# VectorE instead of GpSimd computes the low parts of the output projection's weights in an attention stage

## The chip, the cores and the metric

The kernel runs on one core of a Trainium2 chip. The metric is device time in microseconds of one execution. One profiled execution of the kernel before gives the trace that is read here. In the trace and below, PE is TensorE (PEld its weight loads), DVE is VectorE, ACT is ScalarE and POOL is GpSimd.

## The reference

One layer of a hybrid decoder is computed for 1024 prompt tokens and 64 sample tokens (8 sequences of 8), all in float32, model width 1024:

```python
def _decoder_layer(x, ...):
    x = _layer_norm(DN_ALPHA * x + 0.5 * _swiglu(x, f1g, f1u, f1d), ...)
    m, s_new, new_k, new_v = _mixer(x, w_in, w_out, gn_w, sinks, ...)
    x = _layer_norm(DN_ALPHA * x + m, ...)
    x = _layer_norm(DN_ALPHA * x + 0.5 * _swiglu(x, f2g, f2u, f2d), ...)

def _mixer(h, w_in, w_out, gn_w, sinks, ...):
    rq, rk, rv, rg, sq, sk, sv = _project_in(h, w_in)
    o_ret, s_new = _retention(rq, rk, rv, s0, RET_CHUNK)
    o_swa = _swa_prompt(sq, sk, sv, sinks)          # window 128, ALiBi, sinks
    y_ret = silu(rg) * _head_group_norm(o_ret, gn_w)
    merged = concatenate([y_ret, o_swa], axis=-1)
    return merged @ w_out, s_new, new_k, new_v
```

The sliding-window attention has 8 query heads on 2 key/value heads. Each block of 128 queries sees its own 128 keys and the 128 before; a learned sink per head joins maximum and denominator of the softmax.

## The kernel before

The layer is a row of stages. Large products are made from float32 numbers that are split in two: a high part, rounded by ACT, and a low part, the raw number minus the high part. A product is high x high + low x high + high x low, so each weight tile needs one rounding and one subtraction before use.

`attention_stage` has a block of its own, and ahead of it and behind it all engines meet. The next block begins with `output_projection_stage`, whose products use `out_weights`. These are eight raw tiles of 128x1024 (`ow_raw`), rounded by `OutWeights.round` on ACT (L1490, to `ow_hi`) and split by `OutWeights.split` (L1494, to `ow_low`). Both run inside the attention stage; the projection's TensorE program waits for all eight low parts before its first product.

The stage works on 18 items: 8 prompt blocks and the sample tokens, each for 2 key/value heads. Items 0 and 1 have no block before theirs and are half as wide; 2 to 15 are whole; 16 and 17 are the samples. An item passes the engines so:

- PE `score` (L1599): scores of 4 heads into PSUM
- DVE `add_bias` (L1670), then `top` (the maximum L1678, and three small operations on 128x4 statistics, L1680, L1682, L1683)
- ACT `exponentials` (L1724)
- DVE `denominator` (L1687, L1689)
- POOL (L1785): the scores times the inverse denominator, in place. It is called norm here
- PE `transposes` (L1619), ACT `read_turned` (L1745), PE `output` (L1640)
- ACT `high_part` (L1760), DVE `low_part` (L1704): the result in two parts

Each engine runs an order written out by hand:

- PE: scores of items 0 to 3; then for each i: transposes(i), score(i+4), output(i-1)
- DVE: for each i from -4: add_bias(i+4), top(i+4), denominator(i+3), low_part(i-2)
- ACT: exponentials 0 to 3; then for each i: read_turned(i), exponentials(i+4), high_part(i-1), and for i below 8 round of weight tile i
- POOL: for each i: norm(i), and for i from 1 to 8 split of weight tile i-1, which waits for that tile's rounding

There are four score buffers (`SLOTS = 4`), two sets of score banks, and two of turned tiles. SP (the DMA queue) loads bias tables, caches and the eight raw tiles at the stage's start and stores the new caches.

Of the kernel before, what the change touches and what calls it, by code (L numbers as in the profile page):

```python
# [22 lines left out]
F32 = mybir.dt.float32  # L23
F32R = mybir.dt.float32r
ACT = mybir.ActivationFunctionType
ALU = mybir.AluOpType
# [5 lines left out]
KT = D_MODEL // P  # L32
# [168 lines left out]
def ffn_stage(core, tag, buffers, w_in, fold, acc, xh, xl, wait_x, acc_ready, norm, room=None, banks_free=None,  # L201
# [161 lines left out]
    def gpsimd_early(pool):  # L363
        split(pool, 0, 0, GATE)
        split(pool, 0, 0, UP)

    def gpsimd(pool):
        def step(f, s):
            split(pool, f + 1, 1 - s, GATE)
            split(pool, f + 1, 1 - s, UP)  # L370
            split(pool, f, s, DOWN)

        step(0, 0)
        if prefetch:
            prefetch.gpsimd_early(pool)
        tiles(pool, step)
        split(pool, B, 1, GATE)
        split(pool, B, 1, UP)
        split(pool, A, 0, DOWN)
        split(pool, B, 1, DOWN)  # L380
        for t in range(7):
            norm.gain(pool, t)
# [1090 lines left out]
class OutWeights:  # L1473
# [15 lines left out]
        act.wait_ge(self.staged[k // 2], 32)  # L1489
        act.activation(self.hi[k][:, :], self.raw[k][:, :], ACT.Copy).then_inc(self.hi_done, 1)  # L1490

    def split(self, pool, k):
        pool.wait_ge(self.hi_done, k + 1)
        pool.tensor_tensor(self.low[k][:, :], self.raw[k][:, :], self.hi[k][:, :].bitcast(F32),  # L1494
                           ALU.subtract).then_inc(self.lo_done, 1)


def attention_stage(core, at, at_caches, tables, sinks, sinks_dec, caches, q_t, k_t, v_tok, ident,
# [36 lines left out]
    def shape(i):  # L1535

        n, h = ITEMS[i]
        if n == BLOCKS:
            return 2, 0, KEYS
        return GROUP, (P if n == 0 else 0), 2 * P  # L1540

    def scores_of(i):
        n, h = ITEMS[i]
        groups, k0, k1 = shape(i)
        width = KEYS if n == BLOCKS else 2 * P
        return scores[i % SLOTS][:, 0:groups * width].rearrange("p (g k) -> p g k", g=groups)[:, :, k0:k1]

    def per_group(i, what):
        return stats[i % SLOTS][:, what, 0:shape(i)[0]]

    def sinks_of(i):
        n, h = ITEMS[i]
        if n == BLOCKS:
            return sinks_dec[:, h:h + 1].to_broadcast([P, 2])
        return sinks[:, GROUP * h:GROUP * h + GROUP]
# [98 lines left out]
    def vector(dve):  # L1654
        def add_bias(i):
            n, h = ITEMS[i]
            groups, k0, k1 = shape(i)
            dve.wait_ge(tables_in if n == BLOCKS else bias_in[h], 16)
            dve.wait_ge(scored, i + 1)
            if i >= SLOTS:  # L1660
                dve.wait_ge(turn_done, i - SLOTS + 1)
            out = scores_of(i)
            if n == BLOCKS:
                ps = score_ps[i % 2][0][:, 0:2 * KEYS].rearrange("p (g k) -> p g k", g=2)
                dve.scalar_tensor_tensor(out, ps, QSCALE, bias_dec[:, h, :, :], ALU.mult, ALU.add)\
                   .then_inc(biased, 1)
            else:
                for j in range(2):
                    ps = score_ps[i % 2][j][:, :].rearrange("p (g k) -> p g k", g=2)[:, :, k0:k1]
                    x = dve.scalar_tensor_tensor(out[:, 2 * j:2 * j + 2, :], ps, QSCALE,  # L1670
                                                 bias[:, h, 2 * j:2 * j + 2, k0:k1], ALU.mult, ALU.add)
                x.then_inc(biased, 1)

        def top(i):
            dve.wait_ge(biased, i + 1)
            if i >= SLOTS:
                dve.wait_ge(normed, i - SLOTS + 1)
            dve.tensor_reduce(per_group(i, TOP), scores_of(i), AX.X, ALU.max).then_inc(maxed, 1)  # L1678
            dve.wait_ge(maxed, i + 1)
            dve.tensor_tensor(per_group(i, TOP), per_group(i, TOP), sinks_of(i), ALU.max).then_inc(topped, 1)  # L1680
            dve.wait_ge(topped, i + 1)
            dve.tensor_tensor(per_group(i, SINK), sinks_of(i), per_group(i, TOP), ALU.subtract)  # L1682
            dve.tensor_scalar(per_group(i, NEG), per_group(i, TOP), -1.0, None, ALU.mult).then_inc(negated, 1)  # L1683

        def denominator(i):
            dve.wait_ge(sink_exped, i + 1)
            dve.tensor_tensor(per_group(i, DEN), per_group(i, SUM), per_group(i, SINK), ALU.add).then_inc(summed, 1)  # L1687
            dve.wait_ge(summed, i + 1)
            dve.reciprocal(per_group(i, INV), per_group(i, DEN)).then_inc(inverted, 1)  # L1689

        def low_part(i):
            n, h = ITEMS[i]
            d = slice(HD * h, HD * h + HD)
            dve.wait_ge(hi_done, i + 1)
            if n == BLOCKS:
                for t in range(GROUP):
                    x = dve.tensor_tensor(
                        mix_lo[d, PAIRS + t, SEQ:TOK].rearrange("p (b i) -> p b i", i=DEC_SEQ),
                        out_ps[h][d, 0:2 * P].rearrange("p (b t i) -> p b t i", t=GROUP, i=DEC_SEQ)[:, :, t, :],
                        mix_hi[d, PAIRS + t, SEQ:TOK].rearrange("p (b i) -> p b i", i=DEC_SEQ).bitcast(F32),  # L1700
                        ALU.subtract)
                x.then_inc(lo_done, 1)
            else:
                dve.tensor_tensor(mix_lo[d, PAIRS:2 * PAIRS, P * n:P * n + P],  # L1704
                                  out_ps[h][d, :].rearrange("p (t q) -> p t q", t=GROUP),
                                  mix_hi[d, PAIRS:2 * PAIRS, P * n:P * n + P].bitcast(F32),
                                  ALU.subtract).then_inc(lo_done, 1)

        for i in range(-SLOTS, LAST + 2):
            if i + SLOTS < LAST:  # L1710
                add_bias(i + SLOTS)
                top(i + SLOTS)
            if 0 <= i + SLOTS - 1 < LAST:
                denominator(i + SLOTS - 1)
            if i >= 2:
                low_part(i - 2)

    def scalar(act):
        def exponentials(i):
# [55 lines left out]
    def gpsimd(pool):  # L1775
        for t in range(GROUP):
            pool.tensor_copy(q_rows[:, :, t, :], q_t[:, t, SEQ:TOK].rearrange("p (b i) -> p b i", i=DEC_SEQ))\
                .then_inc(q_ordered, 1)
        pool.memset(turned_new[:, :], 0.0).then_inc(q_ordered, 1)
        for i in range(LAST):  # L1780
            n, h = ITEMS[i]
            groups, k0, k1 = shape(i)
            pool.wait_ge(inverted, i + 1)
            s = scores_of(i)
            pool.tensor_tensor(s, s, per_group(i, INV).unsqueeze(2).to_broadcast([P, groups, k1 - k0]),  # L1785
                               ALU.mult).then_inc(normed, 1)
            if 1 <= i <= KT:
                out_weights.split(pool, i - 1)

    return Stage(sync=sync, tensor=tensor, vector=vector, scalar=scalar, gpsimd=gpsimd)  # L1790


# [109 lines left out]
def decoder_layer(core, i, o):  # L1902
# [84 lines left out]
    with nc.Block() as block:  # L1987
# [48 lines left out]
        def _(pe):  # L2036
# [5 lines left out]
        core, att_end, mix_lo_att_at, gates_end, i["gn_sum"], i["gn_spread"], ones_head, eps, part("gn_w"), ret_q, ret_gate,  # L2042
        mix_hi, mix_lo, i["w_att"], xh, xl, ident, att_q, att_k, att_v_tok, retention.outputs_stored))
    one_stage_block(nc, attention_stage(core, att_end, mixer_at, i, part("sinks"), part("sinks_dec"),
                                        {"k": i["k_cache"], "v": i["v_cache"]}, att_q, att_k, att_v_tok, ident,
                                        mix_hi, mix_lo, o, out_weights))
# [202 lines left out]
```

## Time and profile before

| what | value |
|---|---|
| time, median of 3 runs | 2267.71 us (2265.05 to 2269.71) |
| the profiled execution's own time | 2266.3 us |
| its span, first to last instruction | 2264.4 us |
| PE busy | 2197.3 us (97% of the span) |
| PEld busy | 1978.2 us (87%) |
| DVE busy | 892.3 us (39%) |
| ACT busy | 510.6 us (23%) |
| POOL busy | 520.2 us (23%) |
| attention stage | from about 1217 to 1340 us of the span |

The span is 1.9 us shorter than the execution's time; that is what lies around it. Busy shares are means over all stages. The attention stage lies in slices 22 to 24 of the 40 that the profile's page draws (each 56.6 us), and in those PE is below nine tenths and its granted clock is below full speed.

### The profile page before, as it was taken

The numbers are of one execution on the slowest core, as the hardware profiler recorded it, in microseconds if no ns is written. First come the engines' busy times: TensorE is split into PE (matmuls) and PEld (weight loads), VectorE is DVE, ScalarE is ACT, GpSimd is POOL, SyncE is SP. The second block draws the span as 40 slices with busy tenths as digits, with TensorE's granted clock in tenths as the row PEclk, the third lists the DMA queues.
The fourth block names the chain that finished last, engine by engine and source line by source line (L and its number), as shares of the span: only waits on it lengthen the run. The fifth ranks groups of instructions, "written<-read, shape, count | busy, mean of one in ns | idle before, by whom it ended". The sixth has DMA issues, their size and how long they took to land. (4 is left out here: it accounts for less than half of the span.)

```text
span 2264.4 us, 31134 instructions
## 1 busy us (share of the span) xinstructions
PE 2197.3 (97%) x12045; PEld 1978.2 (87%) x12045; DVE 892.3 (39%) x1606; ACT 510.6 (23%) x877; POOL 520.2 (23%) x253
## 2 busy tenths in 40 slices
PE   8999999999999999999898889999999999999997
PEld 8999999999999889996676458799999999999996
DVE  5534434344344430012133543433443434435246
ACT  4111111111111431111123542311111111111115
POOL 4121221212212222213122522222112121221213
PEclk9999999999999999999697699999999999999999
DMA  7101011010111011110103030010101101010112
GB/s 271 56 28 56 28 56 49 34 56 28 56 42 52 29 70 66 37 32 21 65 10 140 0 114 3 29 56 28 56 28 56 46 37 56 28 56 28 56 57 79
DMA packets 37817, 118.42 MB, mean 52 GB/s; under 512 B 5879, under 2 KB 10615, under 8 KB 37503
## 3 DMA queue, kind: packets, MB, share of 16 engines
q1 hardware_dynamic: 37759, 117.61, 14.6%
q8 instruction: 41, 0.67, 0.1%
q14 instruction: 17, 0.14, 0.0%
HBM read 106.32 MB, written 11.27 MB: 52 GB/s over the span
## 5 line engine op out<-in xcount | busy, mean ns | idle before, releaser
L111 PE MATMUL bank<-x_hi,f_w_hi 128*128 128x362 f32 (+1 forms) x2104 | 688.3, 327 | 7.0 <-issue 5.6
L113 PE MATMUL bank<-x_hi,f_w_low 128*128 128x362 f32 (+1 forms) x2104 | 689.9, 328 | 0.0
L360 POOL TENSOR_TENSOR f_w_low<-f_w_raw,f_w_hi 128x1024 fp32r<-128x1024 f32 x132 | 317.3, 2418 | 1177.5 <-ACT f_w_hi L290 1177.5
L548 DVE TENSOR_TENSOR acc<-bank,acc 128x512 f32<-128x512 f32 x720 | 468.0, 687 | 7.0 <-PE bank L446 5.8
L111 PEld LDWEIGHTS bank<-x_hi,f_w_hi 128*128 128x128 f32 x2104 | 396.4, 188 | 9.1 <-issue 7.4
L113 PEld LDWEIGHTS bank<-x_hi,f_w_low 128*128 128x128 f32 x2104 | 395.9, 188 | 0.0
L526 DVE TENSOR_TENSOR f_h_full<-bank,f_silu 128x362 f32<-128x362 f32 (+1 forms) x132 | 70.7, 535 | 816.9 <-PE bank L113 814.6
L112 PE MATMUL bank<-x_lo,f_w_hi 128*128 128x362 f32 (+1 forms) x1056 | 345.3, 327 | 0.0
L112 PE MATMUL bank<-x_low,f_w_hi 128*128 128x362 f32 (+1 forms) x1048 | 342.9, 327 | 0.0
L444 PE MATMUL bank<-f_w_hi,f_h_hi 128*128 128x512 f32 x640 | 250.8, 392 | 0.1
L446 PE MATMUL bank<-f_w_low,f_h_hi 128*128 128x512 f32 x640 | 250.1, 391 | 0.0
L445 PE MATMUL bank<-f_w_hi,f_h_lo 128*128 128x512 f32 x640 | 249.9, 390 | 0.0
L299 ACT ACTIVATE f_silu<-bank 128x362 f32<-128x362 f32 (+1 forms) x132 | 62.5, 474 | 682.4 <-PE bank L113 682.4
L112 PEld LDWEIGHTS bank<-x_lo,f_w_hi 128*128 128x128 f32 x1056 | 198.9, 188 | 0.9
L112 PEld LDWEIGHTS bank<-x_low,f_w_hi 128*128 128x128 f32 x1048 | 197.2, 188 | 0.8
L305 ACT ACTIVATE f_h_hi<-f_h_full 128x362 fp32r<-128x362 f32 (+1 forms) x132 | 67.0, 508 | 528.8 <-DVE f_h_full L526 528.8
L446 PEld LDWEIGHTS bank<-f_w_low,f_h_hi 128*128 128x128 f32 x640 | 120.1, 188 | 26.7
L444 PEld LDWEIGHTS bank<-f_w_hi,f_h_hi 128*128 128x128 f32 x640 | 120.1, 188 | 25.1 <-issue 0.8
L445 PEld LDWEIGHTS bank<-f_w_hi,f_h_lo 128*128 128x128 f32 x640 | 120.1, 188 | 24.6
L290 ACT ACTIVATE f_w_hi<-f_w_raw 128x1024 fp32r<-128x1024 f32 x132 | 134.0, 1044 | 32.3 <-DMA f_w_raw<-ffn_in 32.3
L111 PE MATMUL bank<-x_hi,rp_w_hi 128*128 128x362 f32 (+1 forms) x384 | 127.0, 331 | 3.9 <-ACTq L908 3.9
L113 PE MATMUL bank<-x_hi,rp_w_low 128*128 128x362 f32 (+1 forms) x384 | 126.3, 329 | 0.0
(192 smaller groups left out, 2347.7 us busy)
## 6 DMA issues: line engine op xcount, KB each, us to landing
f_w_raw<-ffn_in SPq DMA_DIRECT2D x132, 512.0 KB, 4.4
rp_w_raw<-w_ret_in SPq DMA_DIRECT2D x16, 512.0 KB, 3.5
acc<-x_rows_in SPq DMA_DIRECT2D x2, 2048.0 KB, 11.1
kept_rows<-acc SPq DMA_DIRECT2D x8, 512.0 KB, 3.0
ow_raw<-w_out_in SPq DMA_DIRECT2D x8, 512.0 KB, 11.3
y_out<-acc SPq DMA_DIRECT2D x8, 512.0 KB, 2.6
n_rows<-ln_rows_in SPq DMA_DIRECT2D x6, 512.0 KB, 7.8
gp_stage<-w_att_in SPq DMA_DIRECT2D x6, 512.0 KB, 3.4
```

Of the source, the lines that this page charges most:

```text
L111: pe.matmul(out, wh, xh, start=first, stop=False)
L112: pe.matmul(out, wh, xl, start=False, stop=False)
L113: return pe.matmul(out, wl, xh, start=False, stop=last)
L290: act.activation(flat(w_hi[s][j]), flat(w_raw[s][j]), ACT.Copy).then_inc(down_hi if j == DOWN else gu_hi, 1)
L299: act.activation(silu[:, buffer_of(f, s, c), 0:b - a], gate_ps[pair_of(f, s, c)][:, 0:b - a], ACT.Silu).then_inc(silu_done, 1)
L305: act.activation(h_hi[s][:, a:b], h_full[:, buffer_of(f, s, c), 0:b - a], ACT.Copy).then_inc(h_hi_done, 1)
L360: pool.tensor_tensor(flat(w_lo[s][j]), flat(w_raw[s][j]), flat(w_hi[s][j]).bitcast(F32), ALU.subtract).then_inc(done, 1)
L444: pe.matmul(out, h_hi[s][:, u], hi, start=True, stop=False)
L445: pe.matmul(out, h_lo[s][:, u], hi, start=False, stop=False)
L446: pe.matmul(out, h_hi[s][:, u], lo, start=False, stop=True).then_inc(down_done, 1)
L526: dve.tensor_tensor(h_full[:, at, 0:b - a], up_ps[pair_of(f, s, c)][:, 0:b - a], silu[:, at, 0:b - a], ALU.mult).then_inc(pair_free, 1)
L548: dve.tensor_tensor(acc[:, t, d], down_ps[(n + 2 * s) % 4][:, :], acc[:, t, d], ALU.add).then_inc(down_free, 1)
```

## The change

`split` is called on DVE instead of POOL. On POOL the call behind norm(i), for i from 1 to 8, is gone. On DVE it stands at the end of the loop's round i, behind low_part(i-2), and still waits for the rounding of weight tile i-1. Operands, their shapes, the semaphores and their counts are the same.

```diff
-    def split(self, pool, k):
-        pool.wait_ge(self.hi_done, k + 1)
-        pool.tensor_tensor(self.low[k][:, :], self.raw[k][:, :], self.hi[k][:, :].bitcast(F32),
-                           ALU.subtract).then_inc(self.lo_done, 1)
+    def split(self, dve, k):
+        dve.wait_ge(self.hi_done, k + 1)
+        dve.tensor_tensor(self.low[k][:, :], self.raw[k][:, :], self.hi[k][:, :].bitcast(F32),
+                          ALU.subtract).then_inc(self.lo_done, 1)
...
             if i >= 2:
                 low_part(i - 2)
+            if 1 <= i <= KT:
+                out_weights.split(dve, i - 1)
...
                                ALU.mult).then_inc(normed, 1)
-            if 1 <= i <= KT:
-                out_weights.split(pool, i - 1)
-
```

## Rows read from the trace of the kernel before

**Rows 1.** The page's head.
```profile
span 2264.4 us, 31134 instructions
```

**Rows 2.** Windows: stretch and length; each engine's busy us (instructions); PEclk; DMA share; GB/s.
```profile
1242.85:1307.58 64.73, 56.45 (x158) 30.18 (x158) 37.05 (x70) 36.78 (x103) 33.13 (x16) 0.69 0.00 1
1307.58:1322.56 14.98, 13.53 (x85) 7.55 (x84) 12.10 (x33) 11.18 (x37) 6.43 (x4) 1.00 0.01 1
```

**Rows 3.** Timeline: start, duration (us), engine, line, operation, shapes, count, idle before and releaser.
```profile
1251.74 0.18 DVE L1689 RECIPROCAL at_stats<-at_stats 128x4 f32<-128x4 f32 x1
...
1263.82 2.34 POOL L1494 TENSOR_TENSOR ow_low<-ow_raw,ow_hi 128x1024 fp32r<-128x1024 f32 x1 [4.00 <-ACT ow_hi L1490]
1266.13 1.89 POOL L1785 TENSOR_TENSOR at_scores<-at_scores,at_stats 128x1024 f32<-128x1024 f32 x1
1268.07 1.09 PE L1619 MATMUL bank<-small,at_scores 128*128 128x128 f32 x8 [3.32 <-POOL at_scores L1785]
...
1279.18 1.04 ACT L1490 ACTIVATE ow_hi<-ow_raw 128x1024 fp32r<-128x1024 f32 x1
1280.30 2.35 POOL L1494 TENSOR_TENSOR ow_low<-ow_raw,ow_hi 128x1024 fp32r<-128x1024 f32 x1 [4.00 <-ACT ow_hi L1490]
```

**Rows 4.** Waits: who waited for whom, us in total, times, longest.
```profile
PEld bank L1619 <- POOL at_scores L1785: 20.1, 8, 4.2
```

**Rows 5.** Two lines of DVE subtractions: ns least/median/most, first and last start, forms.
```profile
L159 DVE TENSOR_TENSOR x_low<-x_raw,x_hi x6: 902/1694/3194, 6.4 to 21.0; 128x724 fp32r<-128x724 f32 x4, 128x2912 fp32r<-128x2912 f32 x1, 128x2896 fp32r<-128x2896 f32 x1
L534 DVE TENSOR_TENSOR f_h_lo<-f_h_full,f_h_hi x132: 457/537/2795, 25.2 to 2237.3; 128x362 fp32r<-128x362 f32 x44, 128x364 fp32r<-128x364 f32 x44, 128x298 fp32r<-128x298 f32 x44
```

**Rows 6.** A line's least/median/most ns, then timeline of DVE and POOL operations that overlap.
```profile
L1682 DVE TENSOR_TENSOR at_stats<-small,at_stats x18: 160/162/1817, 1222.7 to 1326.0; 128x4 f32<-128x4 f32 x16, 128x2 f32<-128x2 f32 x2
...
1266.22 1.82 DVE L1682 TENSOR_TENSOR at_stats<-small,at_stats 128x4 f32<-128x4 f32 x1
1418.99 1.28 DVE L711 SCALAR_TENSOR_TENSOR acc<-acc,n_stats,n_rows 128x1024 f32<-128x1024 f32 x1
1419.47 3.06 POOL L689 TENSOR_TENSOR acc<-acc,n_rows 128x1024 f32<-128x1024 f32 x1 [9.04 <-ACT acc L682]
```

**Rows 7.** Timeline of DVE's loop round i = 9, and the norm it releases.
```profile
1305.89 1.29 DVE L1670 SCALAR_TENSOR_TENSOR at_scores<-bank,at_bias 128x512 f32<-128x512 f32 x2 [1.92 <-PE bank L1599]
1309.01 0.18 DVE L1689 RECIPROCAL at_stats<-at_stats 128x4 f32<-128x4 f32 x1
1309.22 0.69 DVE L1704 TENSOR_TENSOR mix_lo<-bank,mix_hi 64x512 fp32r<-64x512 f32 x1
1309.26 1.89 POOL L1785 TENSOR_TENSOR at_scores<-at_scores,at_stats 128x1024 f32<-128x1024 f32 x1 [3.89 <-DVE at_stats L1689]
```

**Rows 8.** Timeline of PE, two items: later one first, at the lower clock.
```profile
1292.83 1.97 PE L1619 MATMUL bank<-small,at_scores 128*128 128x128 f32 x8 [0.78 <-POOL at_scores L1785]
1294.73 3.78 PE L1599 MATMUL bank<-att_k,att_q 64*128 64x256 f32 x8
1298.44 3.67 PE L1640 MATMUL bank<-at_turned,att_v_tok 128*64 128x512 f32 x4
...
1277.37 1.99 PE L1599 MATMUL bank<-att_k,att_q 64*128 64x256 f32 x8
1279.29 1.93 PE L1640 MATMUL bank<-at_turned,att_v_tok 128*64 128x512 f32 x4
```

**Rows 9.** Windows, columns as in group 2: where the granted clock moves, and later.
```profile
1258.00:1260.00 2.00, 1.96 (x4) 0.36 (x3) 1.90 (x5) 0.00 (x0) 1.82 (x1) 0.70 0.00 0
1268.00:1270.00 2.00, 1.93 (x11) 1.65 (x12) 0.93 (x5) 1.85 (x7) 0.02 (x1) 0.86 0.00 0
1303.60:1338.00 34.40, 32.45 (x210) 17.69 (x210) 20.07 (x54) 24.34 (x77) 11.00 (x7) 1.00 0.01 1
```

**Rows 10.** Timeline around the first split: output(0) on PE, add_bias(5) on DVE.
```profile
1239.50 1.97 PE L1640 MATMUL bank<-at_turned,att_v_tok 128*64 128x512 f32 x2
1239.67 1.29 DVE L1670 SCALAR_TENSOR_TENSOR at_scores<-bank,at_bias 128x512 f32<-128x512 f32 x2 [4.03 <-PE bank L1599]
```

## The prediction

> **What bounds the kernel now.** I read the page's head first: the span is 2264.4 us [rows 1], 1.9 us under the execution's own 2266.3 us. PE is busy for 97% of it, so anything worth having in this change lies in the one stage that the diff touches, where PE is not full. The windows show that stage in two halves [rows 2]. From 1242.85 us (the transposes of item 2) to 1307.58 (those of item 10) eight items take 64.73 us, 8.1 us each, at a mean granted clock of 0.69. Behind them, from 1307.58 to 1322.56, three items take 14.98 us, 5.0 us each, at the full clock. The first half is the one in which weight tiles are rounded and split.
>
> Then the timeline of that half, to see what turns it [rows 3]. One ring closes over two items: the split of tile 3 starts at 1263.82 on POOL; behind it norm(5) runs from 1266.13; PE, idle for 3.32 us, starts transposes(5) at 1268.07, when norm(5) ends; then come score(9), add_bias(9), its maximum and exponentials, high_part(4), ACT's rounding of tile 5 at 1279.18, and the split of tile 5 at 1280.30. That is 16.48 us for two items. norm(5) needed nothing from this ring: item 5 had its inverse denominator at 1251.9. It stood in POOL's queue behind a split that waits for a rounding, which stands in ACT's queue behind the exponentials of an item four further on. The list of waits shows the price: PE's weight loads for the transposes waited for norm 8 times, 20.1 us together [rows 4], and these gaps also cost clock (below). The split's 2.35 us is the smaller half of its harm; its wait is the larger.
>
> **What goes.** POOL loses 8 x 2.35 us and 8 waits. Norm(i) then starts as soon as its denominator is there, two to three items ahead of its transposes, and is no longer late for PE. In these eight items POOL keeps 1.89 us an item.
>
> **What comes, on DVE.** Eight subtractions of 128x1024 with both inputs in SBUF. The trace before has no such shape on DVE. The nearest rows are 0.902 us for 724 columns and 0.537 for 362 [rows 5], 1.01 ns a column, which gives 1.20 us for 1024; the step from 298 to 362 columns (0.457 to 0.537, 1.25 ns a column) would give 1.37. I take 1.22, nearer to the wider row. The new wait for the rounding is free: ACT rounds tile i-1 straight behind high_part(i-2), and DVE stands behind low_part(i-2), 0.69 us of work, and (next step) behind a norm as well. Were it not, add_bias and top of the next item would be queued behind it, and with them ACT's exponentials.
>
> The costly part is when the subtraction may run. DVE's small two-input operation at 1266.22 took 1.82 us where the median of its line is 0.162, and ended with the norm of 1266.13; the other way round, POOL's addition that came up at 1419.47, while a DVE operation of 1.28 us had been running since 1418.99, took 3.06 us: 0.80 us of waiting and 2.26 of its own [rows 6]. So such operations take turns. Where would the split fall? DVE's round i = 9 shows it [rows 7]: add_bias starts at 1305.89, the reciprocal ends at 1309.19, which releases a norm at 1309.26 to 1311.15, and low_part ends at 1309.91. A split there would find the norm running, start at about 1311.2 and end at 1312.4. The round would take 1312.4 - 1305.9 = 6.5 us, against 4.0 without the split (1309.9 - 1305.9) and 5.2 with a split that met nobody.
>
> The Trainium skill's page "SBUF — State Buffer", section "Who interferes with whom", says the same: a VectorE instruction with two SBUF inputs contends with a GpSimd instruction that reads SBUF, and who is first keeps the port for the whole instruction. It speaks against moving this operation to VectorE; by it the split costs VectorE 2.5 us an item, and by instruction length alone 1.2.
>
> **PE and ACT beside it.** Gapless, an item costs PE at the lower clock 1.97 for transposes, 3.78 for the score and 3.67 for the output, less an overlap of 0.07 at each of the three seams (1292.83 + 1.97 is 0.07 beyond 1294.73): 9.2 us [rows 8]. At the full clock it is 1.09 + 1.99 + 1.93 less the same, 4.8 us [rows 3, 8]. ACT was busy for 36.78 us in eight items, 4.6 us each [rows 2], the rounding included. So at the full clock DVE's 6.5 us sets the pace, at the lower one PE's 9.2.
>
> The clock rose from 1.2 to 2.4 GHz in the window 1258 to 1260, in which PE was busy for 1.96 of 2 us; it fell in the window 1268 to 1270, behind the gap of 3.32 us; from 1303.6 to 1338 PE was busy for 32.45 of 34.40 us and it stayed at full [rows 9]. In the new kernel PE works without a gap as long as it is the slower one, so the clock should rise in item 2, 3 or 4; afterwards PE idles 6.5 - 4.8 = 1.7 us an item, in a gap half as long as the one behind which it fell. I take it that it stays up.
>
> **The sum.** Nothing changes up to output(0) at 1239.50 and add_bias(5) at 1239.67 [rows 10]. Transposes(2) then follow output(0) at 1241.5 instead of 1242.85. With score(6) still at the lower clock (1.90 + 3.70), add_bias(6) starts at 1247.2 From there seven rounds of 6.5 us lead to add_bias(13) at 1247.2 + 45.5 = 1292.7. Before, that was 1305.89 [rows 7]: 13.2 us earlier. Behind it both kernels run the same rounds at about 5 us, and the stage's end and the whole projection follow as much earlier. 2266.3 - 13.2 = 2253.1 us. The median of the runs shown is 1.4 us above this execution (2254.5 by it); I forecast 2254.0.
>
> Bounds of this sum: clock up within item 2, as early as transposes(2): 2.5 us more gain; clock up one or two items later: 9.2 - 6.5 = 2.7 us less gain each; the subtraction at 1.37 us: 7 x 0.15 = 1 us less. The next block starts with its own clock step, which can fall otherwise by 1 or 2 us. So 2249 to 2260.
>
> **Rivals.**
> A. The subtraction does not meet the norm (it goes first, or they don't exclude each other at this shape). A round is 5.2 us: 7 x 1.3 = 9 us more, 2244 us. Against it: [rows 6, 7]. 6%.
> B. The clock keeps swinging as before, because of the 1.7 us gaps, or rises three to six items late: half of the seven rounds at 9.2 us cost 9.5 us, gain 4 us, 2262 to 2267. For it: before, the clock rose and fell within these items and its mean was 0.69 [rows 2, 9]. Against it: the gaps are half as long. 9%.
> C. The clock stays at 1.2 GHz through all seven rounds. PE is then the bound: add_bias(13) at 1247.2 + 7 x 9.2 = 1311.6, 5.7 us later than before, 2272 us, slower. It decides from the fifth slow round on (13.2 / 2.7 = 4.9). For it: at the item of 1292.83 to 1302 the clock was still low, although PE had been busy for most of the stretch before [rows 2, 8]. Against it: PE is without a gap there, and before, it rose in such a stretch [rows 9]. 6%.
>
> **Chances.** Forecast 79%, A 6%, B 9%, C 6%. The median before tells 0.2% (4.5 us), about what a measurement of this kernel can tell from no change. Faster by more than that, under 2263.2: forecast, A and little of B, 85%; the same: most of B, 9%; slower: C, 6%. The range for 8 in 10 is 2248 to 2261: the forecast's own bounds, and a bit of either side.
>
> **What the profile after would show.** Norm with no wait for a split, PE's waits for norm gone; ow_low on DVE x8 at about 2.4 us each (1.2 of it standing behind a norm); add_bias starts 6.5 us apart for items 6 to 13; clock at 1.00 from about 1250 on; DVE's small operations on statistics back at 0.16 us. Starts about 5.2 us apart would speak for A, a clock under 0.9 between 1250 and 1290 for B or C. The forecast is wrong if the stage's end moves by under 8 us or over 18.

## The result, and the profile after

The changed kernel takes 2247.60 us (median of 4 runs, 2243.67 to 2249.86); the kernel before took 2268.11 us beside it (4 runs, 2265.05 to 2269.71). The ratio is 0.9909, with an interval of 0.9896 to 0.9922. The profiled execution took 2248.2 us, against 2266.3. So the gain is 18 us in the profiled pair and 20.5 in the medians, where 13.2 was forecast. The time lies 0.4 us under the lower end of the range. That is less than the kernel's own spread: its repetition a1, below, has 2250.01 us, which lies inside.

The page's head, and its lines of busy time and granted clock (tenths in 40 slices) after the change:

```profile
span 2246.4 us, 31134 instructions
...
PE 2182.5 (97%) x12045; PEld 1973.3 (88%) x12045; DVE 895.3 (40%) x1614; ACT 510.4 (23%) x877; POOL 508.5 (23%) x245
...
PEclk9999999999999999999698899999999999999999
```

VectorE has only 3 us more to do than before, although it took over eight whole tiles, 12.9 us of splits: it got most of that back from two small operations, L1680 and L1682, which had stood waiting for 8.9 us in all. The window from transposes(2) to transposes(10), columns as in [rows 2], is 47.80 us long where it was 64.73, and its clock rose from 0.69 to 0.91:

```profile
1240.66:1288.46 47.80, 42.03 (x160) 23.66 (x159) 41.91 (x80) 36.65 (x103) 21.97 (x8) 0.91 0.00 1
```

The waits that answer to [rows 4], with the total in us, the number and the longest. Two of the waits for norm are left, ahead of items 1 and 15. In items 2 to 9, which had seven of the eight waits before (19.3 of the 20.1 us), there is none. There PE now waits for ACT's reading of the turned tile.

```profile
PEld bank L1619 <- POOL at_scores L1787: 4.0, 2, 3.2
PE bank L1619 <- ACT at_turned L1747: 9.5, 8, 2.5
```

Two rounds of the changed kernel, from the timeline of VectorE and GpSimd (they answer to [rows 3, 7]; norm is now L1787):

```profile
1257.46 1.22 DVE L1678 TENSOR_REDUCE at_stats<-at_scores 128x4 f32<-128x1024 f32 x1
1258.91 0.16 DVE L1682 TENSOR_TENSOR at_stats<-small,at_stats 128x4 f32<-128x4 f32 x1
1259.34 0.65 DVE L1704 TENSOR_TENSOR mix_lo<-bank,mix_hi 64x512 fp32r<-64x512 f32 x1
1259.51 3.38 POOL L1787 TENSOR_TENSOR at_scores<-at_scores,at_stats 128x1024 f32<-128x1024 f32 x1 [4.49 <-DVE at_stats L1689]
1259.92 1.21 DVE L1494 TENSOR_TENSOR ow_low<-ow_raw,ow_hi 128x1024 fp32r<-128x1024 f32 x1
1261.05 1.27 DVE L1670 SCALAR_TENSOR_TENSOR at_scores<-bank,at_bias 128x512 f32<-128x512 f32 x2
...
1264.36 0.69 DVE L1704 TENSOR_TENSOR mix_lo<-bank,mix_hi 64x512 fp32r<-64x512 f32 x1
1264.41 1.89 POOL L1787 TENSOR_TENSOR at_scores<-at_scores,at_stats 128x1024 f32<-128x1024 f32 x1 [1.53 <-DVE at_stats L1689]
1265.09 2.30 DVE L1494 TENSOR_TENSOR ow_low<-ow_raw,ow_hi 128x1024 fp32r<-128x1024 f32 x1
1267.42 1.29 DVE L1670 SCALAR_TENSOR_TENSOR at_scores<-bank,at_bias 128x512 f32<-128x512 f32 x2
```

Norm and split meet in every round, as forecast, and take turns. But in one round the split goes through in 1.21 us and norm is stretched to 3.38, and in the next norm takes its 1.89 and the split 2.30. The rounds last 6.37 and 4.92 us in turn: 11.29 us for two, not 13.0.

A yardstick for all that follows is the stretch from add_bias(5) to add_bias(13), eight rounds. Before: 1239.67 to 1305.89, 66.2 us [rows 7, 10]. After: 1238.92 to 1286.76, 47.8 us. That is 18.4 us less, about the whole gain of the profiled pair: the changed kernel came to this stretch 0.7 us earlier, and lost 1.1 us again behind the stage. The forecast had 53.0 (1292.7 - 1239.67).

### The profile page after: what moved, and what is told of

Same layout as the page of the kernel before. It is cut to its first block and busy times, and to the rows that moved or that the text cites. A ratio compares the mean times of both kernels' runs of the same rounds, so it can differ in the third digit from the quotient of the medians.

```text
span 2246.4 us, 31134 instructions
## 1 busy us (share of the span) xinstructions
PE 2182.5 (97%) x12045; PEld 1973.3 (88%) x12045; DVE 895.3 (40%) x1614; ACT 510.4 (23%) x877; POOL 508.5 (23%) x245
## 5 line engine op out<-in xcount | busy, mean ns | idle before, releaser
L112 PE MATMUL bank<-x_low,rp_w_hi 128*128 128x362 f32 (+1 forms) x384 | 126.5, 330 | 0.0
## 6 DMA issues: line engine op xcount, KB each, us to landing
ow_raw<-w_out_in SPq DMA_DIRECT2D x8, 512.0 KB, 11.3
```

The costliest lines, as they stand in the source:

```text
L112: pe.matmul(out, wh, xl, start=False, stop=False)
```

## Experiments

Each kernel is the changed one or the one before with a single edit, unless said otherwise. The table gathers them: "eight rounds" is the yardstick read from each timeline, "clock falls" those inside it. The kernel before had, beside a1, e1, e2 and e4, a median of 2267.93 us (9 runs), beside e7 to e10 2268.52 (13 runs), beside e5 and e6 a single 2272.85, beside t2 to t4 a single 2267.99.

| kernel | time, us | ratio to before [interval] | eight rounds, us | clock falls |
|---|---|---|---|---|
| before | 2268.11 | | 66.2 | swings throughout |
| changed | 2247.60 | 0.9909 [0.9896, 0.9922] | 47.8 | 1 |
| a1, changed again | 2250.01 | 0.9912 [0.9895, 0.9929] | 49.5 | 2 |
| e1 | 2245.26 | 0.9900 [0.9881, 0.9920] | 44.5 | 0 |
| e2 | 2248.41 | 0.9915 [0.9899, 0.9932] | 46.2 | 1 |
| e4 | 2250.05 | 0.9921 [0.9902, 0.9939] | 49.5 | 2 |
| e5 / e6 | 2259.92 / 2262.00 (one execution each) | | 60.5 / 60.5 | 2 / 1 |
| e7 | 2267.36 | 0.9994 [0.9984, 1.0004] | 64.3 | 0 from 1260 us on |
| e8 | 2242.28 | 0.9883 [0.9866, 0.9899] | 43.0 | 1, short |
| e9 | 2254.73 | 0.9942 [0.9926, 0.9959] | 53.6 | 3 |
| e10 | 2241.68 | 0.9881 [0.9864, 0.9897] | 40.6 | 0 |
| t2 / t3 / t4 | 2249.53 / 2248.34 / 2248.15 (one execution each) | | 50.5 / 47.9 / 49.7 | 1 / 1 / 2 |

**a1, the changed kernel once more.** It gives the spread of the changed kernel itself.

> The changed kernel once more, as a yardstick beside the variants. Expected: 18 to 22 us below the kernel before (2246 to 2250 us), ow_low alternately about 1.2 and 2.3 us long on DVE, longest pauses of PE about 1.4 to 1.8 us. If the gain of 20 us were chance of one chip, it would come out at 13.

The ratio repeats. The same kernel had two clock falls instead of one, and 1.7 us more in the eight rounds.

**e2, was it the place in the queue or the engine?** The kernel before, GpSimd keeps all splits, but each stands behind a later norm, when its rounding is long done:

```diff
-            if 1 <= i <= KT:
-                out_weights.split(pool, i - 1)
+            if 4 <= i < KT + 4:
+                out_weights.split(pool, i - 4)
```

> The kernel before, with all splits on GpSimd, but that of tile i-4 behind norm(i), for i from 4 to 11, in place of tile i-1 for i from 1 to 8. The rounding is then done long before. Theory W (the wait and where it stands is what costs): norm is never late, DVE's statistics are never held for long, and the kernel is as fast as the changed one or up to 3 us faster, 2244 to 2249 us, although GpSimd does just as much. Theory L (GpSimd's length costs: 2.35 + 1.89 us an item, during which DVE's two-input operations stand): DVE's statistics are held by 1 to 2 us an item, and it stays above 2255 us.

```profile
1261.31 0.16 DVE L1682 TENSOR_TENSOR at_stats<-small,at_stats 128x4 f32<-128x4 f32 x1
1261.91 1.89 POOL L1785 TENSOR_TENSOR at_scores<-at_scores,at_stats 128x1024 f32<-128x1024 f32 x1 [2.99 <-DVE at_stats L1689]
1263.76 2.37 POOL L1494 TENSOR_TENSOR ow_low<-ow_raw,ow_hi 128x1024 fp32r<-128x1024 f32 x1
1266.18 0.16 DVE L1682 TENSOR_TENSOR at_stats<-small,at_stats 128x4 f32<-128x4 f32 x1
```

GpSimd's splits cost 2.35 to 2.37 us as before, and yet the time is that of the changed kernel. Norm follows its denominator, the split has no wait, and no small operation of VectorE is held (L1682 takes 0.16 us throughout). What the change brings, it brings by moving the wait out from ahead of norm, not by using a faster engine.

**e4, what do the splits cost VectorE?** The changed kernel without any split. The projection waits for the high parts alone and uses them in place of the low parts too, so its output is another one.

> The splits are left out and the projection's third product takes the high part of the weights a second time (same count of products, other numbers). What the splits still cost in the changed kernel. If only the port and DVE's time bind there, a round falls to the 5.0 to 5.4 us that PE and ACT need, 3 to 4 us less in all: 2244 to 2246 us, equal to the two variants. If DVE were the sole bound, DVE rounds of 4.0 us: over 8 us less, under 2240 us.

The time is that of the changed kernel, where 3 to 4 us less was expected. Without a single split VectorE's round is as short as it can be, and still the rounds are 4.81 and 6.44 us (add_bias at 1257.88, 1262.69, 1269.13, 1273.94): 11.25 us for two. So the changed kernel is not bound by VectorE's 6.5 us a round, which was my step. A ring over two items binds it.

**e1, what if the split never loses the port?** The split goes ahead of `low_part` in VectorE's round, where it starts before norm:

```diff
-            if i >= 2:
-                low_part(i - 2)
             if 1 <= i <= KT:
                 out_weights.split(dve, i - 1)
+            if i >= 2:
+                low_part(i - 2)
```

> DVE does the split ahead of low_part instead of behind it. Theory H (hold): behind a low_part of partitions 64 to 127 the split, which starts at partition 0, is held until low_part has ended, and the norm, released by the reciprocal, gets the port first; behind a low_part of partitions 0 to 63 it isn't held and gets the port first. With nothing between reciprocal and split, all eight splits then take about 1.2 us and all eight norms beside them 2.8 to 3.4 us; add_bias starts 5.0 to 5.7 us apart, the stage ends 3 us earlier than in the changed kernel, 2244 to 2246 us. Theory C (a cycle of two rounds in the timing, whatever lies between): splits stay alternately at 1.2 and 2.3 us, and the time is that of the changed kernel.

```profile
1258.12 1.19 DVE L1494 TENSOR_TENSOR ow_low<-ow_raw,ow_hi 128x1024 fp32r<-128x1024 f32 x1
1258.28 2.78 POOL L1787 TENSOR_TENSOR at_scores<-at_scores,at_stats 128x1024 f32<-128x1024 f32 x1 [3.48 <-DVE at_stats L1689]
...
1263.02 1.20 DVE L1494 TENSOR_TENSOR ow_low<-ow_raw,ow_hi 128x1024 fp32r<-128x1024 f32 x1
1263.08 1.06 PE L1619 MATMUL bank<-small,at_scores 128*128 128x128 f32 x8 [1.13 <-ACT at_turned L1747]
1263.19 2.78 POOL L1787 TENSOR_TENSOR at_scores<-at_scores,at_stats 128x1024 f32<-128x1024 f32 x1 [2.12 <-DVE at_stats L1689]
```

A window of e1, columns as in [rows 2]:

```profile
1242.00:1316.00 74.00, 65.60 (x354) 36.74 (x352) 54.19 (x125) 57.06 (x168) 30.68 (x14) 1.00 0.00 1
```

All splits take 1.2 us, and the pace stays (add_bias at 1248.66, 1254.90, 1259.83, 1266.16: 11.2 us for two). PE's pause ahead of the transposes of items 3 to 9 is 1.13 us at most where the changed kernel shows up to 1.73, and in this window the clock never falls. Both halves of the expectation for H came out, the short splits and the time; theory C did not. The 3.3 us less in the eight rounds are about the price of the changed kernel's one fall (3.1, below). In the medians e1 is 2.3 us under the changed kernel; their intervals overlap.

**The ring of the changed kernel.** From its timeline, over two items: transposes at 1264.31, score 1265.30, add_bias 1267.42, maximum 1268.74, exponentials 1270.47, high_part 1272.66, rounding 1273.28, read_turned 1274.36, transposes 1275.59. That is 11.28 us, through PE, DVE and ACT.

```profile
1264.31 1.06 PE L1619 MATMUL bank<-small,at_scores 128*128 128x128 f32 x8 [1.73 <-ACT at_turned L1747]
...
1273.28 1.06 ACT L1490 ACTIVATE ow_hi<-ow_raw 128x1024 fp32r<-128x1024 f32 x1
1274.36 1.08 ACT L1747 ACTIVATE at_turned<-bank 128x512 f32<-128x512 f32 x2
1275.59 1.06 PE L1619 MATMUL bank<-small,at_scores 128*128 128x128 f32 x8 [1.63 <-ACT at_turned L1747]
```

The rounding of a weight tile stands in ACT's queue between two of its links. If this ring binds, rounding elsewhere must shorten two rounds by about 1.0 us, to 10.3.

**e8 and e10, the rounding out of the ring.** e8 is e1, e10 is e2, each with this edit in ACT's loop:

```diff
             if i < LAST:
                 read_turned(i)
+            if i < KT:
+                out_weights.round(act, i)
             if i + SLOTS < LAST:
                 exponentials(i + SLOTS)
             if i:
                 high_part(i - 1)
-            if i < KT:
-                out_weights.round(act, i)
```

> The variant with the split ahead of low_part, and on ACT the rounding of tile i directly behind read_turned(i), ahead of exponentials(i+4), where ACT waits for DVE's statistics anyway. Theory R (the changed kernel is bound by a ring over two items through all engines: transposes, score, add_bias, maximum, exponentials, high_part, rounding, read_turned, transposes, 11.3 us): 1.04 us of rounding leaves the ring, rounds fall from 5.6 to about 5.2 us, which is then DVE with its split; 3 us less than the variant before it, 2242 to 2245 us. Theory D (DVE's rounds are the bound already): no change against it, 2245 to 2248 us.

> Splits on GpSimd, late (tile i-4 behind norm(i), for i from 4 to 11), and the rounding ahead of exponentials(i+4). No step of the weights is left in any ring; rounds of 5.0 us set by PE, ACT and the statistics. The fastest of all: 2241 to 2244 us. If GpSimd's 4.24 us an item hold DVE's statistics at the port, 2246 us or more.

e8: rounds of 5.25 and 4.95 us, 10.2 for two. e10: 5.36 and 4.81 (add_bias at 1255.90, 1260.71, 1266.07), 10.17 for two, with the splits on GpSimd. Both agree with the ring. e10, at 2241.68 us, has the lowest median of the study, not told apart from e8's; all its executions are below all of the changed kernel's, and it doesn't contain the change.

**What bound the kernel before?** The forecast named a ring over two items through PE, 16.48 us. Read again, the same stretch of the trace before has a shorter one, over one item and without PE: split at 1263.82; norm 1266.13 to 1268.02; VectorE's small operation L1682, held from 1266.22 to 1268.04 [rows 6]; and then, from the timeline of the kernel before (its last line, of the next item, is explained below):

```profile
1268.15 0.51 ACT L1724 ACTIVATE at_scores<-at_scores,at_stats 128x256 f32<-128x256 f32 x1 [3.45 <-DVE at_stats L1683]
1270.35 0.59 ACT L1760 ACTIVATE mix_hi<-bank 64x512 fp32r<-64x512 f32 x1
1270.96 1.06 ACT L1490 ACTIVATE ow_hi<-ow_raw 128x1024 fp32r<-128x1024 f32 x1
...
1272.10 2.35 POOL L1494 TENSOR_TENSOR ow_low<-ow_raw,ow_hi 128x1024 fp32r<-128x1024 f32 x1 [4.08 <-ACT ow_hi L1490]
...
1275.22 1.09 DVE L1680 TENSOR_TENSOR at_stats<-at_stats,small 128x4 f32<-128x4 f32 x1
```

Exponentials, high_part, rounding, next split: 1272.10 - 1263.82 = 8.28 us an item. The link that I had missed is a 128x4 operation that waits for norm at the port. In the next item it is L1680 that is held: it comes up at 1275.22 and ends at 1276.31, with the norm of 1274.40 to 1276.29. Twice 8.28 is 16.56, so my ring had nearly the same length. But it reaches the statistics through add_bias(9) at 1272.65, and L1680 of that item could have been done 0.9 us sooner than the norm let it: my ring had slack there. Both rings contain exponentials, high_part and rounding. e7 tells them apart, and with them the clock; e9 takes the link out that they share.

**e7, more work and a full clock.** The kernel before with the output products of items 2 to 8 computed twice into the same bank:

```diff
-                for kb in range(first, 2):
-                    mm = pe.matmul(out_ps[h][d, :], ...)
+                for turn in range(2 if 2 <= i <= 8 else 1):
+                    for kb in range(first, 2):
+                        mm = pe.matmul(out_ps[h][d, :], ...)
```

> The kernel before, in which PE issues the products of output(i) twice for items 2 to 8 (the second pass starts anew and gives the same numbers), into its idle stretches: 7 x 1.9 us more PE work at the full clock. It asks what the low clock cost. The granted clock should stay near 1.0 from item 3 on. Theory S (PE's steps lie in the ring of the kernel before, as the prediction had it): transposes of 1.09 us in place of 1.97 and scores of 1.99 in place of 3.5 shorten every ring of two items by 1.5 us or more, 4 to 6 us less in all. Theory P (the ring runs GpSimd's split, norm, DVE's held statistics, ACT's exponentials, high_part, rounding, 8.2 us an item, with no PE step in it): rounds stay at 8.2 us, time the same within 3 us, or a little longer.

A window, and three lines of the timeline:

```profile
1260.00:1308.00 48.00, 41.65 (x156) 20.97 (x155) 33.77 (x55) 28.45 (x83) 26.15 (x13) 1.00 0.00 1
```

```profile
1271.58 2.36 POOL L1494 TENSOR_TENSOR ow_low<-ow_raw,ow_hi 128x1024 fp32r<-128x1024 f32 x1 [4.28 <-ACT ow_hi L1490]
1273.89 1.89 POOL L1786 TENSOR_TENSOR at_scores<-at_scores,at_stats 128x1024 f32<-128x1024 f32 x1
1273.99 1.82 DVE L1683 TENSOR_TENSOR at_stats<-small,at_stats 128x4 f32<-128x4 f32 x1
```

The clock is 1.00 for 48 us, the transposes take 1.09 us each, and the splits still start at 1263.10, 1271.58, 1279.60, 1287.88 and 1295.89, 8.0 to 8.5 us apart. The time doesn't change (0.9994, within 0.16% either way). PE's own part of my ring, from transposes(5) to add_bias(9), shrank from 4.58 us (1268.07 to 1272.65) to 3.11 (1267.45 to 1270.56), and the pace of the splits stayed at 8.3 us. So neither PE's work nor its low clock set the pace before: the ring through the port did. Only behind the last split did the full clock count: the eight rounds are 1.9 us shorter than before, 1.7 of them between that split and add_bias(13).

**e9, the kernel before with the rounding early.** Only e8's edit of ACT, splits as before.

> The kernel before, splits on GpSimd as they were, with only ACT's rounding moved ahead of exponentials(i+4). If the wait for the rounding is what closes the ring of the kernel before (split waits for rounding, rounding for exponentials, these for statistics that stand behind GpSimd's norm at the port, norm behind the split), the ring opens: about 10 us less, 2255 to 2260 us. If GpSimd's length is what costs (2.35 + 1.89 us an item), nothing changes: 2266 to 2270 us.

13.8 us less than before, a little more than was expected, without touching any split or GpSimd. Small operations are still held (L1682: 1.82 us at 1256.12) and GpSimd still waits for roundings (4.97, 0.53, 4.77, 0.53 us in turn), but the rounding no longer stands behind exponentials and high_part, and the ring opens: 6.7 us a round. That is still longer than the changed kernel's 5.6 in undisturbed rounds; norm still stands behind a split here, and I take that for the reason, without a run that shows it.

**Who gets the port?** In the changed kernel the split wins in every second round. `low_part` writes partitions 0 to 63 for one key/value head and 64 to 127 for the other; the split, on all 128, starts at partition 0. Hypothesis (H in the expectations): an operation that starts at other partitions than the one ahead is held until that one has ended, and the held split loses the port to norm. The start times fit: behind `low_part` on 0 to 63 the split starts 0.07 us before its end (1259.92 against 1259.99), behind 64 to 127 0.04 after (1265.09 against 1265.05). e5 and e6 cut every split in two halves of 64 partitions. For tiles 2, 4 and 6, whose `low_part` ahead lies on partitions 64 to 127, e5 puts the upper half first and e6 the lower one; the other tiles have the lower half first in both:

```diff
-        dve.tensor_tensor(self.low[k][:, :], ...)
+        for h in (1, 0) if k in (2, 4, 6) else (0, 1):     # e6: (0, 1) for all
+            p = slice(HD * h, HD * h + HD)
+            x = dve.tensor_tensor(self.low[k][p, :], ...)
```

> The changed kernel with each split done in two operations of 64 partitions, 1.2 us each; for tiles 2, 4 and 6, whose low_part in front of them lies on partitions 64 to 127, the upper half goes first. Theory H (an operation that starts at another partition than the one before it is held until that one has ended): the upper half isn't held behind low_part, DVE gets the port first in all eight rounds, the norms of all eight rounds wait for it (2.8 us or more), and no half of a split is longer than about 1.3 us. Theory C (the order at the port alternates by timing alone): norms of 1.89 us appear in some of the rounds of tiles 2, 4 and 6 with a first half of about 2.3 us.

> The same with the lower half first for every tile: the same two operations and the same time on DVE, only the order of the halves differs for tiles 2, 4 and 6. Theory H: behind the low_parts of partitions 64 to 127 the lower half is held, the norm goes first (1.89 us) and the first half of tiles 2, 4 and 6 takes about 2.3 us. Theory C: as in the variant with the upper half first.

H's expectation for e5 failed. For e6 it came out in tiles 2, 4 and 6 (norm 1.89 us, first half 2.29), but the other tiles lose there too. Norm keeps its 1.89 us from the second round on in both kernels, also where the first half is not held (in e5 at 1257.06, 0.07 us before `low_part`'s end): a pair of halves then takes 3.52 to 3.79 us, which is two operations at the whole one's 1.2 us and a wait for norm. All rounds from add_bias(6) on are 7.6 us. Two things could spoil this test: two operations in place of one, or 64 partitions. t4 cuts by columns instead, two operations of 128x512:

```diff
-        dve.tensor_tensor(self.low[k][:, :], ...)
+        for c in (slice(0, 512), slice(512, 1024)):
+            x = dve.tensor_tensor(self.low[k][:, c], ...)
```

> The changed kernel with each split in two operations of 128 partitions and 512 columns, about 0.65 us each. In the two variants that split by partitions the norm went first in every round from the second on. If the partitions (64 in place of 128) were the reason, DVE gets the port first here in every second round, as in the changed kernel (norms of 2.5 us or more there). If the reason is that the operation that waits for the rounding is no longer the one that signals the end, or that there are two, the norm goes first here too, 1.89 us in all these rounds.

From the second on the pairs take 1.27 us with norm at 3.45, and 2.36 with norm at 1.90, in turn, as in the changed kernel. So it is not the count of operations; a form with 64 partitions loses. Why it does stays open. t2 and t3 leave the split whole and put a 64x4 memset of 0.06 us between `low_part` on partitions 0 to 63 and the split, on the upper partitions in t2 and on the lower in t3:

```diff
+            if 2 <= i <= KT and i % 2 == 0:
+                dve.memset(scratch[slice(HD, P), :], 0.0)   # t3: slice(0, HD)
             if 1 <= i <= KT:
                 out_weights.split(dve, i - 1)
```

> The changed kernel with a memset of 4 columns between low_part and split in the rounds whose low_part lies on partitions 0 to 63, the memset on partitions 64 to 127. Theory H (an operation that starts at another partition than the one before is held until that one has ended, and a held split loses the port): now the split is held in these rounds too, the norm goes first in all rounds from the second on (1.89 us), and these splits take 2.2 us or more. If the hold doesn't matter: norms of about 3.4 us in every second round, as in the changed kernel.

> The same memset in the same rounds, but on partitions 0 to 63, where low_part and split start as well. Theory H: nothing is held, DVE keeps the port in these rounds, splits of 1.2 us and norms of 3.4 us in every second round, as in the changed kernel. If it is the extra operation between the two and not where it lies, this looks like the variant with the memset on the upper partitions.

The same round, t2 first, then t3:

```profile
1247.95 1.89 POOL L1790 TENSOR_TENSOR at_scores<-at_scores,at_stats 128x1024 f32<-128x1024 f32 x1 [3.02 <-DVE at_stats L1690]
1248.50 0.06 DVE L1719 MEMSET at_scratch<- 64x4 f32 x1
1248.57 2.35 DVE L1494 TENSOR_TENSOR ow_low<-ow_raw,ow_hi 128x1024 fp32r<-128x1024 f32 x1
```

```profile
1248.09 3.39 POOL L1790 TENSOR_TENSOR at_scores<-at_scores,at_stats 128x1024 f32<-128x1024 f32 x1 [3.06 <-DVE at_stats L1690]
1248.51 1.21 DVE L1494 TENSOR_TENSOR ow_low<-ow_raw,ow_hi 128x1024 fp32r<-128x1024 f32 x1
1248.53 0.06 DVE L1719 MEMSET at_scratch<- 64x4 f32 x1
```

The kernels differ only in which partitions the memset clears, and the split wins in the one and loses in the other. (In t3 the split's record starts even 0.02 us before that of the memset ahead of it.) In t2 it loses in every round from the second on, 2.35 and 2.30 us. That the memset's partitions turn it is shown for the whole split. That the hold is the reason fits, and t4 fits too, but a rival stands: by the records the whole split and t4's first piece start 0.41 to 0.43 us behind norm where they win (the first round aside), and 0.62 us or more behind it where they lose, and no run here delays the split without a hold. e5 and e6 show that neither is the only reason: halves at 0.41 us, not held, lose as well.

t2 is also the kernel that the forecast described: every split behind a running norm. Its seven rounds from add_bias(6) to add_bias(13) take 44.7 us (1244.58 to 1289.26), where the forecast had 45.5.

## Why the prediction was right or wrong

**Right.** The direction. That the harm lay in the split's wait ahead of norm (e2: same gain on the old engine). The split's own price, 1.22 us forecast and 1.21 measured when it wins, 2.3 when it loses against 2.4. That the wait for the rounding is free: the list of waits shows none at it. That norm and split take turns. That PE's waits for norm vanish in items 2 to 9 and L1682 is back at 0.16 us. Transposes(2), forecast at 1241.5, started at 1240.66 in a stage that itself began 0.7 us earlier (GpSimd's first copy at 1216.31 instead of 1216.99): 1241.3 on the old scale.

**The stretch up to add_bias(6).** Forecast 7.5 us from add_bias(5) (1239.67 to 1247.2), measured 5.84 (1238.92 to 1244.76). The clock rose within the window of 1242 to 1244, in item 2. This was the bound "clock up within item 2, 2.5 us more gain", of which 1.7 us came.

**The seven rounds of 6.5 us.** This is the term that was mis-sized: 45.5 us forecast, 42.0 measured (1244.76 to 1286.76). The two items together are 1.7 + 3.5 = 5.2 us, all that the eight rounds differ from the forecast (53.0 against 47.8). The wrong step was "a split there would find the norm running", taken from one round of the trace before [rows 7] for all rounds. That round, i = 9, has an odd item in `low_part`, the case where the split does lose; in the even case it wins, and a round of 4.92 us follows the 6.37. Against it also stood a limit that the forecast didn't have: even with no split the ring over two items allows only 5.6 us a round (e4). So rival A's 5.2 us a round was out of reach, although half of its condition came true. The 3.5 us are the net of two things: undisturbed, the seven rounds would have taken 38.9 us, 6.6 less than forecast, and one fall of the clock, which the sum doesn't have (next paragraph), gave 3.1 back. That the number came so near is in part luck.

**"I take it that it stays up."** Not quite. The clock fell once, in the windows from 1276 to 1284, behind PE's pause of 1.63 us ahead of the transposes at 1275.59, although it had stood through pauses of 1.41 and 1.73 before. PE's timeline, and two windows:

```profile
1276.59 3.44 PE L1599 MATMUL bank<-att_k,att_q 64*128 64x256 f32 x8
1279.95 3.67 PE L1640 MATMUL bank<-at_turned,att_v_tok 128*64 128x512 f32 x4
```

```profile
1276.00:1278.00 2.00, 2.00 (x10) 1.62 (x9) 1.97 (x2) 2.00 (x9) 1.59 (x1) 0.74 0.00 0
1280.00:1282.00 2.00, 2.00 (x4) 0.70 (x4) 1.85 (x3) 0.00 (x0) 0.00 (x0) 0.50 0.00 0
```

At 1.2 GHz score and output took 3.44 and 3.67 us instead of 1.99 and 1.93, and two rounds took 14.4 us (1272.34 to 1286.76) instead of 11.3: 3.1 us. a1 and e4 had two such falls, in 49.5 us each, against 44.7 undisturbed (5.84 + 38.87, seven rounds alternating 5.00 or 4.92 with 6.37): 2.4 us each. In t2 a fall cost 0.5 us in two rounds (13.13 against 12.63): VectorE was the bound there and PE had time. That is a good part of why t2, with every split losing, took only 2.6 us more in the eight rounds (50.5 against 47.8) and 1.3 us more in its one execution.

**What bound the kernel before.** The named ring was not the one that bound (e7), and the sum survived it, since it sets a worked-out stretch against the measured 1305.89 and never uses the ring. Its conclusion also held, because norm behind the waiting split is a link of both rings. But with the wrong ring went the reading that PE's low clock was part of the price before; e7 shows that for the pace of the splits it was not. In the changed kernel the clock does count, as rivals B and C have it: PE is in its ring, and one fall cost 3.1 us. [rows 4] also hold one wait of 0.8 us outside the eight items, ahead of item 15.

**The range.** The sum's bounds reached 2249 and the range 2248, with "clock earlier" in the sum and "the split goes first" only in a rival with a fixed 5.2 us for all rounds. Both happened in part. The profiled execution, 2248.2 us, is 4.9 us under the sum's 2253.1: about 5.2 from the eight rounds and 0.7 from the earlier start, less 1.1 behind the stage. The forecast then added 0.9 us for the median, and the median came out 0.6 under the profiled execution; that is spread of the runs, and with it the time passes the end by 0.4 us. The prediction's own sign speaks as plainly: the stage's end moved by 19.1 us (the last `low_part` from 1339.33 to 1320.19), over the 18 that it allowed, of which 0.7 arose before the stage. A rival that can come true in half of the rounds belongs into the range with half its price: half of its 9.1 us off 2253.1 gives 2248.6, and 2246.1 with the early clock.

## What to carry to other kernels

An instruction that waits at the head of an in-order queue costs all that stands behind it; look for another place for the waiting step on its own engine first. Here that (e2) gave about the same as the faster engine, and one moved ACT operation on top (e10) gave 6.7 us more in the medians. When a ring is named as the bound, look for a shorter one of the same pace, through ports as well as through semaphores, and test it by changing one engine's part of it: where the pace stays although that part got shorter, as PE's in e7, that engine was not in the ring that binds.

## What the runs showed of the hardware

**A tiny operation pays for a big neighbour.** A 128x4 operation of VectorE with two SBUF inputs takes 0.16 us alone and took 1.82 when it came up 0.1 us behind GpSimd's 1.89 us norm (e7, 1273.99), with ACT's exponentials behind it.

**Recorded starts don't tell who has the port.** In the changed kernel norm's record starts at 1259.51 and the split's at 1259.92, yet norm is the one that is stretched, by 1.49 us. It ends 1.76 us behind the split's end, as it does in e1 (1.75), where it starts behind the split: it can have done little in its first 0.41 us. The Trainium skill's page "SBUF — State Buffer", section "Who interferes with whom", has the first comer keep the port for its whole instruction. e1 agrees: a split that starts 0.16 us before norm takes 1.19 us and norm 2.78. The changed kernel doesn't, if the first comer is read from the recorded starts.

**The partitions of the operation ahead matter.** Moving a 0.06 us memset from partitions 0-63 to 64-127 turned the split behind it from 1.21 to 2.35 us and norm from 3.39 to 1.89 (t3, t2). Halves of 64 partitions lost in every round but the first, whichever came first (e5, e6). The reason for either is open.
